# Sampled attention in row and column tiles: new keys on four row quarters, rotary scores in 64 rows

## The reference, cut to what matters

```
q_lat = einsum('bqhd,chd->bqhc', q_nope, w_uk)            # per head: 32 queries x 512 latent channels
s = (einsum('bqhc,bkc->bhqk', q_lat, ckv_all)             # 544 keys = 512 cached + 32 new
   + einsum('bqhr,bkr->bhqk', q_pe, kpe_all)) * SCALE     # the rotary part: 64 channels
p = softmax(s)                                            # no mask bites for the sample frames
o_lat = einsum('bhqk,bkc->bqhc', p, ckv_all)              # contraction over the 544 keys
o = einsum('bqhc,chv->bqhv', o_lat, w_uv)
```

## Time and profile before

| | |
|---|---|
| Time, median of 3 runs | 857.95 us (857.86 to 858.18) |
| The profiled execution: time, span | 857.47 us, 855.7 us |
| PE busy | 828.9 us, 97% of the span |
| PE weight loads busy | 787.1 us, 92% |
| DVE busy | 568.5 us, 66% |
| ACT busy | 471.3 us, 55% |
| POOL busy | 79.7 us, 9% |
| The chain that ended last | PE 83%, ACT 6%, DVE 6%, DMA 2% |

### The profile page before, as it was taken

One profiled execution on the slowest core, in us unless ns is written; L12 is line 12 of the kernel. 1 busy time (PEld: TensorE's weight loads), 2 busy tenths in 40 slices (PEclk: granted clock), 3 DMA queues, 4 the chain that ended last, 5 costly groups with the idle time before them and its releaser, 6 DMA issues.

```text
span 855.7 us, 15623 instructions
## 1 busy us (share of the span) xinstructions
PE 828.9 (97%) x6359; PEld 787.1 (92%) x6359; DVE 568.5 (66%) x947; ACT 471.3 (55%) x817; POOL 79.7 (9%) x144
## 2 busy tenths in 40 slices
PE   6989999999999999999999999999999999999994
PEld 5988999999899899889998999999999999999994
DVE  5676756655565664886759677676679788755554
ACT  5674546466565466655464455444456888733432
POOL 0053002011011011100000000000000000001112
PEclk9999999999999999999999999999999999999998
DMA  7457325326325423434444353455554545545531
GB/s 289 126 178 291 103 82 176 107 62 196 121 74 173 124 74 116 143 117 124 142 119 140 113 151 114 134 205 165 160 168 149 171 158 164 164 159 172 170 126 56
DMA packets 34183, 123.57 MB, mean 144 GB/s; under 512 B 4224, under 2 KB 4368, under 8 KB 33856
## 3 DMA queue, kind: packets, MB, share of 16 engines
q1 hardware_dynamic: 30816, 110.67, 40.1%
q0 software_dynamic: 3104, 11.24, 3.8%
q10 hardware_dynamic: 192, 0.66, 0.2%
HBM read 118.52 MB, written 4.04 MB: 143 GB/s over the span
## 4 chain that ended last, share of the span: by engine, by line
PE 83%; ACT 6%; DVE 6%; DMA 2%; issue 1%; POOL 1%; ACTq 0%; DVEq 0%; POOLq 0%
PE ps_acc L426 15%; PE ps_acc L428 14%; PE ps_acc L427 14%; PE ps_row L428 3%; PE ps_row L426 3%; PE ps_row L427 3%; PE ps_s L611 3%; PE ps_cb L428 2%; PE ps_tr L428 2%; PE ps_tr L426 2%; PE ps_cb L426 2%; PE ps_tr L427 2%; PE ps_cb L427 2%; ACT prob L1026 2%; DVE wlo L1300 1%; DMA wraw<-in_wst 1%
## 5 line engine op out<-in xcount | busy, mean ns | idle before, releaser
L1300 DVE TENSOR_TENSOR wlo<-wraw,whi 128x1024 fp32r<-128x1024 f32 x204 | 249.4, 1225 | 189.5 <-ACT whi L908 189.1
L908 ACT CAST whi<-wraw 128x1024 fp32r<-128x1024 f32 x204 | 213.2, 1046 | 127.4 <-DMA wraw<-in_wst 126.9
L426 PE MATMUL ps_acc<-xh,whi 128*128 128x288 f32 x576 | 178.2, 309 | 8.3 <-DVE wlo L1300 8.3
L428 PE MATMUL ps_acc<-xh,wlo 128*128 128x288 f32 x576 | 171.0, 297 | 0.0
L427 PE MATMUL ps_acc<-xl,whi 128*128 128x288 f32 x576 | 169.1, 294 | 0.0
L426 PEld LDWEIGHTS ps_acc<-xh,whi 128*128 128x128 f32 x576 | 109.0, 189 | 15.0 <-DVE wlo L1300 8.3
L427 PEld LDWEIGHTS ps_acc<-xl,whi 128*128 128x128 f32 x576 | 110.1, 191 | 0.6
L428 PEld LDWEIGHTS ps_acc<-xh,wlo 128*128 128x128 f32 x576 | 108.8, 189 | 0.0
L1349 DVE SCALAR_TENSOR_TENSOR cv<-xp,vec,cv 128x292 f32<-128x292 f32 x96 | 50.3, 524 | 9.1 <-ACT cv L973 6.7
L426 PE MATMUL ps_acc<-o_h,whi 128*128 128x288 f32 x128 | 39.9, 311 | 0.0
L1875 POOL COPY cnew<-xp 128x6 f32<-128x6 f32 x32 | 15.4, 480 | 241.8 <-ACT xp L970 241.8
(11 more groups left out here) (431 smaller groups left out, 2245.5 us busy)
## 6 DMA issues: line engine op xcount, KB each, us to landing
wraw<-in_wst SPq DMA_DIRECT2D x204, 512.0 KB, 3.5
side<-in_ukT POOLq DMA_DIRECT2D x8, 256.0 KB, 3.8
side_v<-in_ukT POOLq DMA_DIRECT2D x8, 256.0 KB, 3.0
out_ssm<-s_out POOLq DMA_DIRECT2D x8, 256.0 KB, 2.5
x<-in_xT SPq DMA_DIRECT2D x2, 576.0 KB, 4.7
ax<-in_xT POOLq DMA_DIRECT2D x1, 1152.0 KB, 6.0
out_y<-d SPq DMA_DIRECT2D x4, 288.0 KB, 2.1
ckvT<-in_cacheT POOLq DMA_DIRECT2D x1, 1024.0 KB, 7.0
```

What stands on the lines that cost most here:

```text
L426: pe.matmul(out, w, mh, start=first, stop=False)
L428: return pe.matmul(out, wl, mh, start=False, stop=last)
L908: act.copy(whi[:, s % RING, :], wraw[:, s % RING, :]).then_inc(split_hi, 1)
L1300: tt(wlo[:, s % RING, :], wraw[:, s % RING, :], whi[:, s % RING, :].bitcast(F32), ALU.subtract).then_inc(split_lo, 1)
```

## The change: what it does

- `sample_scores`: the two products per bank with `kall` become eight products in all, each with 64 contraction rows and 32 weight columns (one head). Heads 0 and 2 use rows 0 to 63, heads 1 and 3 rows 64 to 127; each head has its own quarter of the output rows. In one turn heads 0 and 2 write bank 0 and heads 1 and 3 bank 1; in the next turn they swap.
- `kall` holds the 64 channels twice (two transfers, not four), `qz` the four heads' rotary queries without zeros, made by eight small copies on POOL, each waiting for the one before; `hmask` is gone.
- `o_latent`: the products over the cached keys write columns 384 to 511 of the four banks `ps_att`, one bank for each block of latent channels, and the four products over the new keys come last, each on its own quarter of the contraction rows and its own bank. For this the new latent rows (`ckvK[:, 4]`) are spread over four row quarters, and the new keys' probabilities are repeated four times (`ssc` gets 128 columns more, `sample_scale` writes them in an instruction of its own), so that the fifth transpose is a full one. `o_latent` also waits for `at_cp`, ACT's copies of the prompt probabilities out of the same banks.
- ACT copies `olat` in three instructions, not one.

```diff
             def sample_scores(i):
...
-                pe.wait_ge(qz_ready, i + 1)
+                pe.wait_ge(qz_ready, 8 * i + 8)
...
-                for j, bank in enumerate((ps_s, ps_ss)):
+                banks = (ps_s, ps_ss)
+                for j, bank in enumerate(banks):
                     keys = slice(j * half, (j + 1) * half)
                     for c in range(RB):
                         pe.matmul(bank[:, 0:half], qlat[:, c, :], ckvT[:, c, keys], start=c == 0, stop=False)
-                    for c in range(2):
-                        mm = pe.matmul(bank[:, 0:half], qz[:, c, :, :].rearrange("p h q -> p (h q)"),
-                                       kall[:, c, keys], start=False, stop=c == 1)
+                for turn in range(2):
+                    for h4 in range(4):
+                        j = (h4 + turn) % 2
+                        r = slice(64 * (h4 % 2), 64 * (h4 % 2) + 64)
+                        mm = pe.matmul(banks[j][32 * h4:32 * h4 + 32, 0:half], qz[r, h4 // 2, :],
+                                       kall[r, j * half:(j + 1) * half], start=False, stop=True)
...
             def turn_sample(i):
                 pe.wait_ge(s_norm, i + 1)
                 for j in range(5):
-                    n = P if j < 4 else DEC_SEQ
-                    mm = pe.transpose(ps_s[:, j * P:(j + 1) * P] if j < 4 else ps_ss[0:DEC_SEQ, 0:P],
-                                      ssc[:, j * P:j * P + n], ident)
-                mm.then_inc(st_done, 1)
+                    if j < 4:
+                        pe.transpose(ps_s[:, j * P:(j + 1) * P], ssc[:, j * P:(j + 1) * P], ident)
+                    else:
+                        pe.transpose(ps_ss[:, 0:P], ssc[:, KEYS:KEYS + P], ident).then_inc(st_done, 1)
 
             def o_latent(i):
                 pe.wait_ge(st_cp, i + 1)
                 pe.wait_ge(ck_cp, 1)
+                pe.wait_ge(at_cp, 4 * i + 4)
                 for c in range(RB):
-                    for j in range(5):
-                        n = P if j < 4 else DEC_SEQ
-                        mm = pe.matmul(ps_s[:, c * P:(c + 1) * P], ckvK[0:n, j, c * P:(c + 1) * P], ssT[0:n, j, :],
-                                       start=j == 0, stop=j == 4)
+                    for j in range(4):
+                        pe.matmul(ps_att[c][:, 384:512], ckvK[:, j, c * P:(c + 1) * P], ssT[:, j, :],
+                                  start=j == 0, stop=False)
+                for c in range(RB):
+                    f = slice(32 * c, 32 * c + 32)
+                    mm = pe.matmul(ps_att[c][:, 384:512], ckvK[f, 4, 0:P], ssT[f, 4, :], start=False, stop=True)
...
# ACT
-                act.copy(olat[:].rearrange("p c q -> p (c q)"), ps_s[:]).then_inc(ol_cp, 1)
+                act.copy(olat[:, 0:2, :], ps_row[:, :, 384:512])
+                act.copy(olat[:, 2, :], ps_cb[:, 384:512])
+                act.copy(olat[:, 3, :], ps_tr[:, 384:512]).then_inc(ol_cp, 1)
...
# DVE
-            dve.tensor_reduce(hmask[:], ident.rearrange("p (h i) -> p h i", h=4), AX, ALU.add).then_inc(setup_done, 1)
...
-                dve.tensor_scalar(ssc[:], ssc[:], stat[:, 3, 8:9], None, ALU.mult).then_inc(s_norm, 1)
+                dve.tensor_scalar(ssc[:, KEYS:KEYS + P].rearrange("p (a k) -> p a k", a=4),
+                                  ssc[:, PAST:KEYS].unsqueeze(1).to_broadcast([P, 4, DEC_SEQ]),
+                                  stat[:, 3, 8:9], None, ALU.mult)
+                dve.tensor_scalar(ssc[:, 0:PAST], ssc[:, 0:PAST], stat[:, 3, 8:9], None, ALU.mult).then_inc(s_norm, 1)
...
-                dve.tensor_copy(ssT[0:DEC_SEQ, 4, :], ps_ss[0:DEC_SEQ, 0:P]).then_inc(st_cp, 1)
+                dve.tensor_copy(ssT[:, 4, :], ps_ss[:, 0:P]).then_inc(st_cp, 1)
...
-                    dve.tensor_copy(ckvK[0:DEC_SEQ, 4, :], ps_s[0:DEC_SEQ, :]).then_inc(ck_cp, 1)
+                    for c in range(RB):
+                        y = dve.tensor_copy(ckvK[32 * c:32 * c + 32, 4, 0:P], ps_s[0:DEC_SEQ, c * P:(c + 1) * P])
+                    y.then_inc(ck_cp, 1)
...
# POOL
-                pool.tensor_copy(kall[f, :, PAST:KEYS], krot[:, :, SEQ:T]).then_inc(kab_done, 1)
+                pool.tensor_copy(kall[f, PAST:KEYS], krot[:, q % 2, SEQ:T]).then_inc(kab_done, 1)
...
-            for q in range(4):
-                pool.dma_start(kall[32 * q:32 * q + 32, :, 0:PAST], kpeT.rearrange("(a p) k -> p a k", a=2)
-                               ).then_inc(kall_in, 16)
+            for r in range(2):
+                pool.dma_start(kall[64 * r:64 * r + 64, 0:PAST], kpeT).then_inc(kall_in, 16)
...
-                pool.tensor_tensor(qz[:], qrot[:, :, SEQ:T].unsqueeze(2).to_broadcast([P, 2, 4, DEC_SEQ]),
-                                   hmask[:].unsqueeze(1).unsqueeze(3).to_broadcast([P, 2, 4, DEC_SEQ]), ALU.mult
-                                   ).then_inc(qz_ready, 1)
+                for h4 in range(4):
+                    for half in range(2):
+                        p0, n = 64 * (h4 % 2) + 32 * half, 8 * i + 2 * h4 + half
+                        if 2 * h4 + half:
+                            pool.wait_ge(qz_ready, n)
+                        pool.tensor_copy(qz[p0:p0 + 32, h4 // 2, :], qrot[32 * h4:32 * h4 + 32, half, SEQ:T]
+                                         ).then_inc(qz_ready, 1)
+                pool.wait_ge(qz_ready, 8 * i + 8)
```

More of the change, by code:

```diff
@@ L181, in layer_program @@
         rows_s = after("rows_s", [2 * HEADS_SSM, HPG, DEC_SEQ], F32R)
-        hmask = after("hmask", [P, 4])
         gbias = after("gbias", [P, 2 * KB])
@@ L188, in layer_program @@
         kab = after("kab", [P, 2, SEQ])
-        kall = after("kall", [P, 2, KEYS])
+        kall = after("kall", [P, KEYS])
         acum_s = after("acum_s", [2 * HEADS_SSM, T], F32R)
@@ L240, in layer_program @@
         kh = after("kh", [P, 4, SEQ])
-        qz = after("qz", [P, 2, 4, DEC_SEQ])
+        qz = after("qz", [P, 2, DEC_SEQ])
         side = after("side", [P, 2, RANK])
@@ L248, in layer_program @@
         olat = at("olat", [P, RB, P], end[0] - RB * P * 4)
-        ssc = after("ssc", [P, KEYS])
+        ssc = after("ssc", [P, KEYS + P])
         ssT = after("ssT", [P, 5, P])
@@ L573, in sample_scores @@
                 pe.wait_ge(qlat_cp, i + 1)
-                pe.wait_ge(qz_ready, i + 1)
+                pe.wait_ge(qz_ready, 8 * i + 8)
                 pe.wait_ge(cache_in, 32)
-                pe.wait_ge(kall_in, 64)
+                pe.wait_ge(kall_in, 32)
                 pe.wait_ge(ckt_cp, 1)
@@ L1032, in sample_exp @@
                 act.wait_ge(samax, i + 1)
-                act.activation(ssc[:], ssc[:], ACT.Exp, bias=stat[:, 1, 8:9],
+                act.activation(ssc[:, 0:KEYS], ssc[:, 0:KEYS], ACT.Exp, bias=stat[:, 1, 8:9],
                                accum_out=stat[:, 2, 8:9]).then_inc(saexp, 1)
@@ L1374, in _ @@
             dve.tensor_copy(ones_r[:], con[0:2 * HEADS_SSM, C_ONE:C_ONE + P])
-            dve.tensor_scalar(gbias[:], v1(V_GATE, 2 * KB), 0.5, None, ALU.mult)
-            dve.tensor_reduce(hmask[:], ident.rearrange("p (h i) -> p h i", h=4), AX, ALU.add).then_inc(setup_done, 1)
+            dve.tensor_scalar(gbias[:], v1(V_GATE, 2 * KB), 0.5, None, ALU.mult).then_inc(setup_done, 1)
             ahead(("c", 1))
@@ L1415, in rotate @@
                     dve.wait_ge(o_done, 4 * i)
-                    dve.wait_ge(qz_ready, i)
+                    dve.wait_ge(qz_ready, 8 * i)
                 else:
@@ L1450, in sample_max @@
                 dve.wait_ge(stat_step, 5 * i + 2)
-                dve.tensor_reduce(stat[:, 0, 8:9], ssc[:], AX, ALU.max).then_inc(stat_step, 1)
+                dve.tensor_reduce(stat[:, 0, 8:9], ssc[:, 0:KEYS], AX, ALU.max).then_inc(stat_step, 1)
                 dve.wait_ge(stat_step, 5 * i + 3)
```

## The result

The changed kernel takes 850.09 us (median of 4 runs, 849.56 to 850.62) where the kernel before takes 857.90 (4 runs, 857.69 to 858.18): ratio 0.9905, 95% interval 0.9893 to 0.9917. It is 7.8 us faster; 8.6 were forecast (849.3, range 846.3 to 853.0). The profiled execution took 850.62, with a span of 848.8 where it was 855.7.

The account below looks back on a forecast made before the run. PE, busy 97% of the span, was taken to bound the kernel. 7.3 us from `o_latent` plus 1.3 from the set-up gave 8.6 us: 848.9 for the profiled execution, 849.3 for the median, range 846.3 to 853.0.

Parts of the forecast that it names:

- o_latent: End of each round's latent products: one excursion to 32 rows instead of four saves 1.82 us a round, 7.3 in all.
- Start of o_latent: Before the first latent pass: DVE's last copy sets the start, and the new wait for `at_cp` costs nothing; 0.
- sample_scores: Score products on PE: section 0.53 us shorter, but PE only waits longer at `turn_probs`; worth 0.
- The serial rival: Score products: 64-row, 32-column tiles run one after another, 5.7 us lost, 855.0 in total; chance 0.07.
- that of the exposed loads: Score products: each small weight load is exposed, making the kernel 3.6 us slower, 861.5; chance 0.06.
- The rival in which the scores pay: Score products: their shortening counts too, 4 x 0.53 = 2.1 us more gained, 847.2; chance 0.09.
- sample_scale, ACT's three copies, POOL's eight: Added work in the rounds on DVE (0.24 us), ACT (0.9 in all) and POOL (about 4): all hidden, 0.
- Set-up: Before the rounds: two transfer starts fewer and smaller `kall` copies on POOL shorten the chain by 1.3 us.
- so all of it moves together: Set-up chain: cache loads sharing engines with the 7.64 us weight transfer follow the same chain, so they shift with it.
- set-up gives nothing: Set-up: the long weight transfer ends when the cache loads end, so only 7.3 us is gained, 850.7; chance 0.14.

Follow-up runs that it names:

- block-by-block kernel: Changed kernel with each quarter-height product of `o_latent` issued right behind its own block of latent channels, four excursions instead of one: 856.51 us, ratio 0.9977.
- the padded one: Changed kernel with the last 32 keys in `o_latent` as full-height products padded with zeros, no narrow product: 850.93 us, ratio 0.9914.
- the other move: Changed kernel with DVE's low part of the weight chunk moved behind `sample_max`, `prob_scale` and `sample_scale`: 845.06 us, ratio 0.9843.

## Why the prediction was right, point by point

- **o_latent** (forecast 1.82 us a round, 7.3 in all): shown. 6.01 to 4.20 in all four rounds, 7.24. The block-by-block kernel gives it back, and the padded one prices the excursion at 0.60.
- **Start of o_latent** (0): the stretch from `turn_probs` is 5.18 after 5.17, DVE's copy sets it as forecast (the new wait of 0.7 us in four at PE's weight loads lengthens it by 0.01). The wait for `at_cp` appears in no row.
- **sample_scores** (0.53 shorter, worth 0): shown. 0.58 shorter, all of it turned into waiting (0.8 to 3.2 us in four at PE), while the chain kept its 12.21; doubling the products cost nothing; with the chain shortened the section pays 0.59. PEld's longest wait is 1.0, as forecast. The serial rival (855.0) and that of the exposed loads (861.5) fall with the timeline: four tiles every 0.24 us. The rival in which the scores pay (847.2) falls too.
- The Trainium skill, TensorE: Matmul & The Clock Gate, Part 3, The mechanism, was cited in the prediction for weight loads that overlap only where the row group differs. The same section names a second case, loads into the background weight buffer. The trace fits this second case, though it can't show the buffer: heads 0 and 2 load on the same 64 rows and start together, and the loads for the next four products start at 96.13 to 96.15, while the first four (from 96.10) still run on these rows.
- **sample_scale, ACT's three copies, POOL's eight** (0 each): 0.29 us on DVE, which is idle for 0.82 behind it; 0.71 us on ACT from 114.08 to 114.79 (0.9 estimated), 4.8 us before `sample_out` needs it; 4.04 on POOL, its state copy done at 77.57 (near 77 forecast).
- **Set-up** (1.3 us): the mis-sized term. POOL's chain from ACT's `xp` copy to the start of the state copy became 1.12 shorter (9.96 to 8.84; nearly all of it the transfer starts, for the four smaller copies into `kall` together gained only 0.1), but ACT's wait only 0.8, because the state copy took 0.51 instead of 0.20. In this one profile the weight transfer took most of the rest back: counted from that `xp` copy (44.61 before, 45.55 after) it started at 27.48 instead of 28.30 and ended at 35.79 instead of 35.94. In the profiled execution 0.14 us are left, over all profiles some 0.6. Two steps of the term were wrong: that ACT gets all that POOL saves, and "so all of it moves together": the transfer's issue moved by 0.8, its end by 0.15 here and by 0.6 on average. The rival "set-up gives nothing" has its mechanism partly borne out, but not its price: about half of the forecast 1.3 arrives.
- **Not in the sum**: the products of `v_part` run 0.16 a round faster, and from `prompt_out` to the next `turn_q_latent` it is 25.34 after 25.44, about 0.95 us over the rounds; the last part is 0.4 longer, which is within what the profiles with the same tiles differ by (525.48 to 526.86).

The profiled executions add up: 7.24 (`o_latent`) + 0.14 (set-up) + 0.95 (pace) - 0.4 (last part) - 0.94 (the first `xp` copy came at 45.55 instead of 44.61, before anything the change touches) = 7.0; the spans differ by 6.9. That late start is one profile against one, and says nothing of the medians. With 0.6 for the set-up, as over all profiles, the terms give 7.24 + 0.6 + 0.95 - 0.4 = 8.4; the ratio says 8.2, with an interval from 7.1 to 9.2 (the medians 7.8). The totals alone therefore could not tell 8.6 from what was measured; that the set-up term was too large is read from the stages. That 8.6 came so near is in part luck: the set-up gave some 0.7 less than forecast, and the pace of `v_part` and its neighbours, which was in no term, gave 0.95 more.

Open: how an address in SBUF sets the pace of a product, and which tiles matter. Not tried: moving one tile alone. The tiles behind `ssc` can hardly matter: in the kernel with the new scores alone they lie 512 bytes lower than in the changed one, and `v_part` takes 5.64 to 5.68 in both. Also open is why the late load of `ckvK` gives 2.0 us in the total where the set-up stretch gains 1.1 to 1.5; with the other move beneath it it gives 2.2 (0.9843 to 0.9817), so something else may gain with it, but intervals of about 1.2 us each way don't settle it.

## What to carry to other kernels

Count the changes of tile height in PE's stream, not the passes: put the narrow products of all blocks behind the full ones, each block in a bank of its own, or pad them, if there are few (6.01 us became 4.20 and 4.49). Before shortening PE work, look for a wait of PE behind it, however short: 0.2 us of wait in each round (0.36 of slack) told that PE wasn't the late one there, and that was enough to make the 0.58 us of saved products worth nothing, until a 1.23 us step of another engine was moved off the chain. And a change of tile sizes can move the time by a third of a per cent by itself; a difference this small between two kernels isn't explained by their instructions alone.

## What of the hardware was not expected

- An unused tile of 16 bytes made a kernel of 858 us slower by 3.1 (1.0036, interval 1.0022 to 1.0050). The mean distance of two passes of `v_part`, each round's first left out, went from 116.9 to 119.1 ns; in the changed kernel it is 113.7.
- 64-row tiles of 32 columns run four at a time, two on the same rows and each on its own columns: 16 passes of 272 columns in about 1.05 us, and with the changes of tile height included the section got 0.58 shorter.
- An excursion to quarter height costs 0.6 us whether it holds two passes (0.60) or eight (0.61).
